# Squares ahead of the scaled copies, single tiles ahead of the pairs: the RMS norms of a two-block layer kernel on one Trainium2 core

## The reference, cut to what matters

```python
def rms_norm(x, g):
    xf = x.astype(F32)
    y = xf * lax.rsqrt(jnp.mean(xf * xf, axis=-1, keepdims=True) + NORM_EPS)
    return (y * g.astype(F32)).astype(x.dtype)

for layer in range(DEPTH):                        # first block
    u = rms_norm(h, norm_mix_g[layer])
    p = u @ w_in[layer]
    ...
    h = h + merged @ w_o[layer]
    u = rms_norm(h, norm_ffn_g[layer])
    h = h + conv_glu(u, w_up[layer], ...)
return rms_norm(h, norm_final_g)

for l in range(DEPTH):                            # second block
    x = x + 0.5 * swiglu(rmsnorm(x, ffn1_norm[l]), ffn1_w_gu[l], ffn1_w_down[l])
    x = x + hybrid_mixer(rmsnorm(x, mix_norm[l]), ...)
    x = x + 0.5 * swiglu(rmsnorm(x, ffn2_norm[l]), ffn2_w_gu[l], ffn2_w_down[l])
return rmsnorm(x, final_norm)
```

## Time and profile before

| what | value |
|---|---|
| median of 3 runs | 3278.16 us |
| the profiled execution, its own time | 3272.9 us |
| its span, first to last instruction | 3271.1 us |
| TensorE matmuls, busy | 2856.0 us, 87% of the span |
| VectorE busy | 1945.2 us, 59% |
| ScalarE busy | 1362.7 us, 42% |
| mean granted clock of TensorE | 0.918 |
| mean DMA rate | 118 GB/s |

### The profile page before, as it was taken

One profiled execution on the slowest core, in us unless ns is written; L12 is line 12 of the kernel. 1 busy time (PEld: TensorE's weight loads), 2 busy tenths in 40 slices (PEclk: granted clock), 3 DMA queues, 4 the chain that ended last, 5 costly groups with the idle time before them and its releaser, 6 DMA issues. The chain is left out here.

```text
span 3271.1 us, 53748 instructions
## 1 busy us (share of the span) xinstructions
PE 2856.0 (87%) x23052; PEld 2442.1 (75%) x23052; DVE 1945.2 (59%) x2620; ACT 1362.7 (42%) x1873; POOL 152.0 (5%) x116
## 2 busy tenths in 40 slices
PE   7888678889898678889998998879999988988899
PEld 6787557778787557778887785668888877756788
DVE  5754766875754766875647444566566564446564
ACT  5413344545413334555544223355454532335453
POOL 0030000000030000000000220000000003100000
PEclk9898888999898888998999898989999989889899
DMA  5211124454211114454543111144655421113353
GB/s 211 91 40 52 65 67 141 164 191 168 91 40 52 65 65 142 158 199 150 204 157 118 47 40 55 62 155 169 222 170 205 145 97 39 65 39 113 134 206 130
DMA packets 54669, 386.19 MB, mean 118 GB/s; under 512 B 6688, under 2 KB 7328, under 8 KB 8352
## 3 DMA queue, kind: packets, MB, share of 16 engines
q1 hardware_dynamic: 54432, 382.76, 33.8%
HBM read 381.69 MB, written 1.05 MB: 117 GB/s over the span
## 5 line engine op out<-in xcount | busy, mean ns | idle before, releaser
L320 PE MATMUL banks<-normed_high,weights_high 128*128 128x256 f16 (+1 forms) x4096 | 1147.8, 280 | 86.3 <-DVE weights_low L306 55.4
L321 PE MATMUL banks<-normed_low,weights_high 128*128 128x256 f16 (+1 forms) x4096 | 1146.5, 280 | 0.0
L322 PE MATMUL banks<-normed_high,weights_low 128*128 128x256 f16 (+1 forms) x4096 | 1145.2, 280 | 0.0
L306 DVE SCALAR_TENSOR_TENSOR weights_low<-weight_ring,weights_high 128x2048 f16<-128x2048 f32 x334 | 761.2, 2281 | 411.2 <-ACT weights_high L300 395.4
L300 ACT ACTIVATE weights_high<-weight_ring 128x2048 f16<-128x2048 f32 x306 | 580.2, 1898 | 291.9 <-PE banks L322 272.3
L320 PE MATMUL banks<-projected,weights_high 128*128 128x256 f16 x1696 | 473.1, 279 | 79.0 <-DVE projected L331 71.9
L320 PEld LDWEIGHTS banks<-normed_high,weights_high 128*128 128x128 f16 (+1 forms) x4096 | 411.3, 100 | 169.5 <-issue 90.4
L321 PE MATMUL banks<-projected,weights_high 128*128 128x256 f16 x1696 | 473.4, 279 | 0.0
L322 PE MATMUL banks<-projected,weights_low 128*128 128x256 f16 x1696 | 473.0, 279 | 0.0
L322 PEld LDWEIGHTS banks<-normed_high,weights_low 128*128 128x128 f16 (+1 forms) x4096 | 410.7, 100 | 58.9
L321 PEld LDWEIGHTS banks<-normed_low,weights_high 128*128 128x128 f16 (+1 forms) x4096 | 410.1, 100 | 57.6 <-issue 1.3
(11 more groups left out here) (391 smaller groups left out, 3260.7 us busy)
## 6 DMA issues: line engine op xcount, KB each, us to landing
weight_ring<-w SPq DMA_DIRECT2D x356, 1024.0 KB, 4.9
small_weights<-small SPq DMA_DIRECT2D x2, 1280.0 KB, 8.6
constants<-const SPq DMA_DIRECT2D x1, 1601.0 KB, 10.1
weight_ring<-w SPq DMA_DIRECT2D x2, 640.0 KB, 3.8
residual<-xt SPq DMA_DIRECT2D x1, 1024.0 KB, 5.1
small_weights<-small SPq DMA_DIRECT2D x2, 512.0 KB, 10.4
out<-residual SPq DMA_DIRECT2D x4, 256.0 KB, 2.8
parameters<-par SPq DMA_DIRECT2D x2, 115.5 KB, 9.4
```

Of the source, the lines that this page charges most:

```text
L306: nc.vector.scalar_tensor_tensor(out=self.part(self.mem.w_low, g), in0=self.part(self.mem.ring, g), scalar=W_SCALE, in1=self.part(self.mem ...
L320: pe.matmul(out, w_high, high, start=start, stop=False, skip_group_check=skip)
L321: pe.matmul(out, w_high, low, start=False, stop=False, skip_group_check=skip)
L322: return pe.matmul(out, w_low, high, start=False, stop=stop, skip_group_check=skip)
```

## The change

In `before_root` the square root on a constant comes ahead of the two weight highs, which are now handed in as a list. With `spaced` False (all norms but `ffn1_*` and `ffn3_*`) both highs come ahead of the squares as they did; `gained(2)` is moved behind `squares(3)`. With `spaced` True (`ffn1_*`, `ffn3_*`) the weight high of job 0 stands behind `gained(0)` and that of job 1 behind `gained(1)`; `squares(2)`, `gained(2)`, `squares(3)` follow. In `ffn_stage` the second early low half, `next_low(dve, 1)`, is moved from behind the first residual to behind the fourth. The chain normed, high, low runs in five pieces in place of four: tile 0 alone, tile 1 alone, then the pairs 2-3, 4-5, 6-7; TensorE waits ahead of tiles 0, 1, 2, 4 and 6. `fin1` and `fin2` keep their pairs.

```diff
--- before.py
+++ after.py
@@ -341,6 +341,8 @@
 class Norm:
 
 
+    PIECES = ((0, 1), (1, 1), (2, 2), (4, 2), (6, 2))
+
     def __init__(self, mem, cut, sig, gain, ready, sums, spread):
         self.mem, self.sig, self.ready = mem, sig, ready
         self.gain, self.sums, self.spread_bank = CG[gain], sums, spread
@@ -367,19 +369,28 @@
                              ACT.Sqrt, scale=1.0 / D, bias=self.mem.c("eps", 1)
                              ).then_inc(self.sig("root"), 1)
 
-    def before_root(self, act, nc):
+    def before_root(self, act, nc, highs, spaced):
+
         nc.scalar.activation(self.unread, self.mem.c("eps", 1), ACT.Sqrt)
+        if not spaced:
+            for high in highs:
+                high(act)
         for b in range(3):
             self.squares(act, nc, b)
-            self.gained(act, nc, b)
+            if b < 2 or spaced:
+                self.gained(act, nc, b)
+            if b < 2 and spaced:
+                highs[b](act)
         self.squares(act, nc, 3)
+        if not spaced:
+            self.gained(act, nc, 2)
         self.root(act, nc)
         self.gained(act, nc, 3)
 
     def highs(self, act, nc):
-        for b in range(4):
-            act.wait_ge(self.sig("normed"), b + 1)
-            nc.scalar.activation(flat(self.two(self.mem.u_high, b)), flat(self.two(self.u, b)),
+        for i, (k, n) in enumerate(self.PIECES):
+            act.wait_ge(self.sig("normed"), i + 1)
+            nc.scalar.activation(flat(self.mem.u_high[:, k:k + n, :]), flat(self.u[:, k:k + n, :]),
                                  ACT.Copy, scale=X_SCALE).then_inc(self.sig("u_high"), 1)
 
     def sum(self, pe):
@@ -403,31 +414,35 @@
         dve.wait_ge(self.sig("root"), 1)
         nc.vector.reciprocal(self.stat, self.stat).then_inc(self.sig("inverse"), 1)
 
-    def normed(self, dve, nc, b, out):
-        dve.wait_ge(self.sig("gained"), b + 1)
-        inverse = self.mem.ps[:, self.spread_bank, 0:T].unsqueeze(1).to_broadcast([P, 2, T])
-        nc.vector.tensor_tensor(self.two(out, b), self.two(self.scaled, b), inverse, ALU.mult
+    def normed(self, dve, nc, k, n, out):
+        dve.wait_ge(self.sig("gained"), k // 2 + 1)
+        inverse = self.mem.ps[:, self.spread_bank, 0:T].unsqueeze(1).to_broadcast([P, n, T])
+        nc.vector.tensor_tensor(out[:, k:k + n, :], self.scaled[:, k:k + n, :], inverse, ALU.mult
                                 ).then_inc(self.sig("normed"), 1)
 
-    def low(self, dve, nc, b):
-        dve.wait_ge(self.sig("u_high"), b + 1)
-        nc.vector.scalar_tensor_tensor(out=flat(self.two(self.mem.u_low, b)),
-                                       in0=flat(self.two(self.u, b)), scalar=X_SCALE,
-                                       in1=flat(self.two(self.mem.u_high, b)), op0=ALU.mult,
+    def low(self, dve, nc, i):
+        k, n = self.PIECES[i]
+        dve.wait_ge(self.sig("u_high"), i + 1)
+        nc.vector.scalar_tensor_tensor(out=flat(self.mem.u_low[:, k:k + n, :]),
+                                       in0=flat(self.u[:, k:k + n, :]), scalar=X_SCALE,
+                                       in1=flat(self.mem.u_high[:, k:k + n, :]), op0=ALU.mult,
                                        op1=ALU.subtract).then_inc(self.sig("u_low"), 1)
 
     def scale(self, dve, nc):
+
         self.inverse(dve, nc)
         dve.wait_ge(self.sig("spread"), 1)
-        for b in range(4):
-            self.normed(dve, nc, b, self.u)
-            if b:
-                self.low(dve, nc, b - 1)
-        self.low(dve, nc, 3)
+        last = len(self.PIECES) - 1
+        self.normed(dve, nc, *self.PIECES[0], self.u)
+        for i in range(last):
+            self.normed(dve, nc, *self.PIECES[i + 1], self.u)
+            self.low(dve, nc, i)
+        self.low(dve, nc, last)
 
     def arrived(self, pe, k):
-        if k % 2 == 0:
-            pe.wait_ge(self.sig("u_low"), k // 2 + 1)
+        at = [first for first, _ in self.PIECES]
+        if k in at:
+            pe.wait_ge(self.sig("u_low"), at.index(k) + 1)
 
 
 
@@ -463,9 +478,8 @@
 
     def scalar(act):
         link, say, need = linker(act, sig, "act_ops")
-        for g in jobs[:2]:
-            stream.high(act, nc, sig, g)
-        norm.before_root(act, nc)
+        norm.before_root(act, nc, [lambda act, g=g: stream.high(act, nc, sig, g)
+                                   for g in jobs[:2]], False)
         norm.highs(act, nc)
         stream.high(act, nc, sig, jobs[2])
         split_up_to = first + 2
@@ -770,7 +784,8 @@
 
 
 
-def ffn_stage(nc, mem, sig, stream, first, gain, ready, spare, conv, factor, loads, next_low):
+def ffn_stage(nc, mem, sig, stream, first, gain, ready, spare, conv, factor, loads, next_low,
+              spaced=True):
 
     cut = Cutter(mem.scratch)
     norm = Norm(mem, cut, sig, gain, ready, *spare)
@@ -810,9 +825,7 @@
 
     def scalar(act):
         link, say, need = linker(act, sig, "act_ops")
-        high(act, 0)
-        high(act, 1)
-        norm.before_root(act, nc)
+        norm.before_root(act, nc, [lambda act: high(act, 0), lambda act: high(act, 1)], spaced)
         norm.highs(act, nc)
         high(act, 2)
         for j in range(PAIRS):
@@ -888,8 +901,7 @@
             say(nc.vector.scalar_tensor_tensor(out=h, in0=mem.ps[:, 4 + b, :],
                                                scalar=factor * PART_H, in1=h, op0=ALU.mult,
                                                op1=ALU.add), "residual")
-            if b == 0:
-                next_low(dve, 1)
+        next_low(dve, 1)
 
     def tensor(pe):
         norm.sum(pe)
@@ -940,13 +952,13 @@
             sp.wait_ge(sig("stored"), 64)
 
     def scalar(act):
-        norm.before_root(act, nc)
+        norm.before_root(act, nc, [], False)
 
     def vector(dve):
         norm.inverse(dve, nc)
         dve.wait_ge(sig("spread"), 1)
         for b in range(4):
-            norm.normed(dve, nc, b, mem.h)
+            norm.normed(dve, nc, 2 * b, 2, mem.h)
             if b % 2:
                 next_low(dve, b // 2)
 
@@ -2876,7 +2888,7 @@
                                          "mix2_%d" % layer, after_residual(f_sig), LOW_SPARE, loaded,
                                          delta, AHEAD)
             ffn, low, _ = ffn_stage(nc, mem, f_sig, stream, base, "ffn2_%d" % layer, ready, spare,
-                                    None, 0.5, loads, low)
+                                    None, 0.5, loads, low, False)
             return ffn, project, low
 
         rwkv = Rwkv(nc, mem, Scoped(sig, "project_"))
```

## The result

The changed kernel takes 3251.82 us, the median of 4 runs (3247.18 to 3255.96), the kernel before in the same comparison 3279.17 (4 runs, 3278.11 to 3281.11). The ratio is 0.9915, with a 95% interval of 0.9899 to 0.9931. The gaps at the norms shrank about as forecast. Nearly as much again came from stretches of the kernel in which the change touches nothing.

A forecast was written before the change was run, and what follows sets the result against it. TensorE, busy 87% of the span, was taken as the bound, through its stalls and low clock at the norms. Gains 2.1 + 3.6 + 1.5 + 7.4 = 14.6 us gave 3258.3 profiled, 3263.6 as median; range 3256.6 to 3271.5.

The forecast's parts named there:

- The sum of the gaps: All norms and the start: gains of 2.1, 3.6, 1.5 and 7.4 us, together 14.6 us less.
- Start: Start of the kernel: one table load goes, squares 1.5 us earlier; pieces bring the first product another 0.74 us forward.
- The pieces: Ten norms' restarts: first product 1.48 us behind the first normed in place of 2.22; 0.74 us each, 7.4 in all.
- squares at the start: ScalarE at the kernel's start: squares at 16.6 in place of 18.09, a gain of 1.5 us.
- a microsecond won ahead of the restart is won at the end: Behind each restart: FFN and projection jobs follow without a gap, so gains stay whole unless TensorE's clock takes them back.
- the mixers' order hangs on the projection's end: Mixers: argument against rival (e), 3%, in which they give the norms' gain back at their next waits, 3278 us.
- (a): Norm restarts: the clock comes back at the same moments as now, 7.3 us of gain left, 3270.9 us; chance 15%.
- (b): Norm restarts: the clock comes back sooner, 3.5 us behind against a mean of 4.9; 7 us more gain, 3256.6; 8%.
- offset: Whole kernel: the shown median lies 5.3 us above the profiled execution, and the same distance was added to 3258.3.
- signs of being wrong: Norms: sum still waits for squares, gaps in the restart, or fewer than 29 to 40 matmuls in 6 us behind it.

The follow-up runs named there:

- e9_after_one: The changed kernel with three copies (1.6 us) on ScalarE ahead of the root of `mix2_1` alone; 3265.07 us, ratio 0.9957 to the kernel before.

## Why the prediction was wrong

**The sum of the gaps was right.** Start: forecast 2.2 us, measured 2.3 (29.84 to 27.59). The pieces: 1.48 us from the first normed to the first product, measured 555.17 - 553.69 = 1.48; squares at the start at 16.6, measured 16.59. Gap by gap, first trace against first trace: `ffn1_0` 1.52 (forecast 1.29), `ffn1_1` 1.50 (1.29), `ffn3_1` 1.25 (1.24), `ffn2_1` 1.58 (1.49), `mix2_1` 1.31 (1.49). Two were sized too high: `mix1_1` 1.31 (1.89) and `ffn3_0` 0.83 (1.24), since the clock fell earlier in the sum than before. `mix2_0` 1.43 (1.69; 2.4 in the second trace, where the clock fell later). `ffn2_0` gave nothing (0.74): the pieces won it, and the sum of `fin1` ahead of it lost it, with the clock falling 2.4 us in:

```profile
1487.64 4.63 PE L401 MATMUL banks<-constants,scratch 128*128 128x2 f32 x32
```

All told 15.0 of 14.6, against the mean of two traces each.

**The step that failed** is "a microsecond won ahead of the restart is won at the end", with its companion under the rivals, that the mixers' order hangs on the projection's end and so gives nothing back. I let the clock act on the 6 us behind a restart only. It acts on the next 500 as well. When a norm lets TensorE restart decides how much low clock the mixers behind it get, over stretches in which TensorE waits often. The windows above show it, at 0.79 against 0.96 in the same place of the same code. The Trainium skill (TensorE: Matmul & The Clock Gate, HAM oscillation — how this bites in real kernels) tells of a kernel whose waits for transfers throw the clock down again and again. The waits here are for VectorE above all (in the stretch of `e9_after_one` 18.2 us in five waits for `projected`, L331, and one of 6.9 us for L2230), and the granted clock falls and rises again in the same manner, 0.65 to 0.96 in the windows.

The stretch behind `mix2_1` takes 490.6 to 503.4 us, by the distance from its restart to the rise of the clock. That a later restart changes it is shown by a delay in that norm alone: upwards beyond doubt in the changed kernel, downwards with less certainty in the kernel before. The distance itself is a sign that goes with the length; no run sets it apart from the moment of the restart. For the other three stretches there are traces only, but those behind `mix2_0`, where the same mixers run, fall in the same bands. The twelve traces without unread products:

| rise behind the restart | behind `mix2_1` | behind `mix2_0` |
|---|---|---|
| 3.0 to 3.1 us | 490.6 to 494.4 us (4 traces) | 490.8 (1) |
| 3.4 to 4.9 | 502.0 to 503.4 (4) | 502.0 to 505.9 (8) |
| 5.2 to 6.0 | 493.6 to 497.1 (4) | 496.3 to 496.8 (3) |

With the products the bands don't hold on: `mix2_0` has 500.1 us with the rise at 1.5.

Of the 28.6 us between the means of the traces (27.3 by the medians), then, 15 are the change's own work, 2.5 come in the FFN stretches, and about 11 are where the mixers happened to fall. That is luck, though the kernel's median repeats it. Over nine restarts the clock is back on average 3.9 us behind the restart in the first changed trace and 4.2 in the second, before 5.0 and 4.3. In the FFN stretches this is all there is: added up over their six restarts the distances are 30.7, 26.4, 22.2 and 25.6 us in the order of the ledger, and with half of that taken off the six stretches come to 1084.9 to 1085.1 us in all four traces. Rivals (a) and (b) were two signs of the same effect, priced at the restarts only, so the range was too narrow. That a kernel with the pairs is as fast as the whole change does not say that the pieces are worth nothing: they shorten the gaps by 6 us and the mixer stretches gave 5 to 12 back.

**What was wrong in the method**: 3272.9 us for the profiled execution stood 5.2 us below the lowest timed run shown, and I carried the distance over as an offset. It was probably a sign of another course of the clock: the second trace has 9.6 us more in the one stretch. Of the 11.8 us by which the forecast missed, 6.1 are this offset (5.3 added; the changed kernel's profiled execution lies 0.8 above its median), and 5.6 lie between the profiled executions (3258.3 forecast, 3252.7 measured). None of my signs of being wrong looked at a stretch that the change doesn't touch, so nearly all came true beside a wrong time (the 6 us behind a restart hold 29 to 44 matmuls, and the sum runs without a wait in all eight norms, in `mix1_1` for 4.6 us and not 4.0).

**Left open**: what ties the length of a stretch to the rise ahead of it, and why the rise falls at the same distance behind a restart in most traces of one kernel, so that its median repeats to 1 us (3251.8 and 3251.1) while kernels differ by 10. Which wait in the mixers tips a spell wasn't tried, nor a delay ahead of the other three mixer stretches.

## What to carry to other kernels

Where an engine's granted clock moves between two levels in the course of a kernel, cut the span at the places the change touches and compare the untouched stretches too: here they moved by as much as the touched ones. A small change to such a kernel needs a delay of the same size as its control, in one place, before its gain is called its own. And idle time of TensorE ahead of a burst can be filled with products that nobody reads: with 2 and 6 of them in each norm the kernel took 10 us less, of which some 4 in the FFN stretches are read as the clock's return at the restarts; the part in the mixers had no such control.

## What the runs showed of the hardware

- 1.6 us of delay on ScalarE in one norm changed the time by 12 to 14 us upwards in one kernel and by 8 (2 to 12 by its interval) downwards in another, the latter within what that kernel's own runs span.
- In the changed kernel the granted clock falls 2.4 to 4.2 us behind the first of the 32 sum matmuls (128x2), while they run back to back or right behind them (they take 3.6 us at the full clock). With four products of 128x256 among them and eight in the waits it stayed at 1.00 through two of the gaps and fell in the others.
- The first table load ran at 0.74 us, 11.6 us ahead of the activation that needs it, in the time of that activation's wait.
- A change of table cost 1.3 us: the squares at the start came 18.09 - 16.59 = 1.5 us earlier, the constant's activation included. The Trainium skill (ScalarE: Activation LUTs, What ACT_TABLE_LOAD costs) has a drain on top, 2.66 us in all. The trace has no room for it: at `ffn1_0` before, the split ends at 546.32, the load starts at 546.33 and the squares at 547.74, 1.41 us behind it, with the constant's activation between the earlier trace rows.
